# Both mixers in two kinds of visits, copies back in place, and a head of joint weight tiles

## What is computed

```
z = rmsnorm(x, g_mix) @ w_in                       # 2048 -> 5632 columns, split among the heads
mixer A: 16 heads x 64; each evaluates three (window, dilation) patterns (128,1), (512,4), (2048,16),
         with ALiBi; the three outputs are mixed by their softmax denominators
mixer B: 16 query heads / 4 kv heads x 64; keys t-128..t, ALiBi, a sink logit in the denominator
h = x + concat(oa * silu(ga), ob * silu(gb)) @ w_out
y = h + (p @ w_ple) * sigmoid(rmsnorm(h, g_ple) @ w_pg);  final rmsnorm
```

## Time and profile before

| | |
|---|---|
| median of 3 runs | 2344.28 us (2338.28 to 2345.48) |
| the profiled execution | 2341.7 us |
| its span, first to last instruction | 2339.9 us |
| TensorE busy | 2278.0 us (97%), mean granted clock 0.995 |
| VectorE, ScalarE, POOL busy | 905.0 us, 565.0 us, 771.8 us |
| TensorE busy in the first 65 us | 34.6 us |
| TensorE busy from 135 to 900 us | 765.0 us of 765.0 |

### The profile page before, as it was taken

How to read it: one execution, slowest core, us unless ns; L and a number is a source line. 1 busy time by engine, 2 the same in 40 slices (tenths; PEclk the granted TensorE clock), 3 DMA queues, 4 the chain that set the end, 5 groups by cost and what they waited for, 6 DMA issues and landing times.

```text
span 2339.9 us, 39175 instructions
## 1 busy us (share of the span) xinstructions
PE 2278.0 (97%) x15570; PEld 2179.3 (93%) x15570; DVE 905.0 (39%) x2334; ACT 565.0 (24%) x1562; POOL 771.8 (33%) x783
## 2 busy tenths in 40 slices
PE   4999999999999999999999999999999999999996
PEld 4999999999999999999988999899999999999996
DVE  7123333333324413455555424343233373222235
ACT  5122222222222212323544310210000030000374
POOL 2232222222222133222222233343333344555564
PEclk9999999999999999999999999999999999999998
DMA  5144454444444425455464454454343555444666
GB/s 196 61 125 96 104 117 96 108 114 96 109 111 96 107 71 147 131 147 146 138 160 142 135 174 131 158 139 111 86 102 92 122 164 133 113 115 109 194 202 224
DMA packets 542140, 299.71 MB, mean 128 GB/s; under 512 B 245140, under 2 KB 507300, under 8 KB 540668
## 3 DMA queue, kind: packets, MB, share of 16 engines
q1 hardware_dynamic: 464277, 254.82, 41.1%
q10 hardware_dynamic: 77680, 42.39, 6.3%
HBM read 230.76 MB, written 66.36 MB: 127 GB/s over the span
## 4 chain that ended last, share of the span: by engine, by line
PE 90%; DVE 4%; DMA 2%; ACT 2%; POOL 1%; issue 0%; SPq 0%; DVEq 0%; ACTq 0%; POOLq 0%
PE psum L1081 26%; PE psum L1083 26%; PE psum L1082 26%; PE psum L889 3%; PE psum L911 2%; PE psum L922 2%; PE psum L951 1%; PE psum L979 1%; PE psum L966 1%; DMA h_stage<-h_scratch 1%; DVE x_n L1554 1%; DVE act_lo L1545 1%; PE psum L986 1%; POOL w_lo L845 0%; DMA x_in<-in_x_prompt 0%; DVE act_lo L1912 0%
## 5 line engine op out<-in xcount | busy, mean ns | idle before, releaser
L1081 PE MATMUL psum<-act_hi,w_hi 128*128 128x344 f32 x4032 | 1303.4, 323 | 6.6 <-POOL w_lo L845 5.3
L1083 PE MATMUL psum<-act_hi,w_lo 128*128 128x344 f32 x4032 | 1286.9, 319 | 0.0
L1082 PE MATMUL psum<-act_lo,w_hi 128*128 128x344 f32 x4032 | 1286.1, 319 | 0.0
L1081 PEld LDWEIGHTS psum<-act_hi,w_hi 128*128 128x128 f32 x4032 | 758.2, 188 | 17.9 <-issue 12.4
L1083 PEld LDWEIGHTS psum<-act_hi,w_lo 128*128 128x128 f32 x4032 | 757.5, 188 | 0.0
L1082 PEld LDWEIGHTS psum<-act_lo,w_hi 128*128 128x128 f32 x4032 | 757.2, 188 | 0.2
L843 POOL CAST w_hi<-w_raw 128x512 fp32r<-128x512 f32 (+1 forms) x352 | 222.8, 633 | 1464.1 <-PE psum L1083 1274.9
L845 POOL TENSOR_TENSOR w_lo<-w_raw,w_hi 128x512 fp32r<-128x512 f32 (+1 forms) x390 | 508.7, 1306 | 59.6 <-ACT w_hi L1488 31.3
L1657 DVE COPY prob_t<-psum 128x512 f32<-128x512 f32 (+1 forms) x56 | 35.5, 634 | 391.5 <-PE psum L922 391.5
L1958 DVE TENSOR_TENSOR t_gate<-psum,acc 128x344 f32<-128x344 f32 x48 | 24.7, 515 | 224.9 <-PE psum L1083 224.9
L1889 DVE TENSOR_TENSOR h_row<-psum,h_row 128x344 f32<-128x344 f32 x48 | 22.1, 513 | 212.9 <-PE psum L1083 212.9
(11 more groups left out here) (208 smaller groups left out, 1787.4 us busy)
## 6 DMA issues: line engine op xcount, KB each, us to landing
w_raw<-in_w_in SPq DMA_DIRECT2D x208, 256.0 KB, 3.0
w_raw<-in_w_pg SPq DMA_DIRECT2D x94, 256.0 KB, 2.8
w_raw<-in_w_out SPq DMA_DIRECT2D x64, 256.0 KB, 2.7
z_scratch<-stage ACTq DMA_DIRECT2D x72, 172.0 KB, 1.9
h_scratch<-h_row ACTq DMA_DIRECT2D x16, 516.0 KB, 2.7
x_in<-in_x_prompt SPq DMA_DIRECT2D x8, 1024.0 KB, 5.1
zq<-z_scratch SPq DMA_DIRECT2D x32, 256.0 KB, 3.9
out<-z_sq SPq DMA_DIRECT2D x128, 64.0 KB, 2.8
```

Source lines behind the costliest of these rows:

```text
L1081: pe.matmul(psum[:, bank, 0:T3], hi_w, hi_a[:, k, rows], start=(k == 0), stop=False, skip_group_check=True)
L1082: pe.matmul(psum[:, bank, 0:T3], hi_w, lo_a[:, k, rows], start=False, stop=False, skip_group_check=True)
L1083: return pe.matmul(psum[:, bank, 0:T3], lo_w, hi_a[:, k, rows], start=False, stop=stop, skip_group_check=True)
```

## The change

- **Mixer A, two kinds of visits.** Chunks 1 and 2, and 3 and 4, are scored in one visit. A pair has eight steps in 144 positions; at even ones TensorE does values and then scores (positions 0, 36, 72, 108 of the pair), at odd ones turns alone (22, 58, 94, 130). A chunk scored at step s is turned at s + 1 (the far chunk, scored at 0, at 7), and its values are done at the next even step. Scores and turns of a chunk use the same PSUM banks (2 and 3, or 4 and 5: `A_SLOT`); outputs collect in banks 6 and 7.
- **Copies back in place.** The turned columns are copied into `prob` where the chunk stood; `prob_t` and `probt_b` are gone, and `prob` has one set of places instead of two.
- **Mixer B.** Four blocks (`BQ`) in a visit: values and scores at steps 0 and 4, turns at 3 and 7. The scores of four blocks go head by head for two blocks each, no longer block by block.
- **Head.** x has three buffers and is normed in place. Three row tiles are turned first; the first unit does high x high and high x low for all k, and low x high behind them. The first two column tiles are walked jointly, third by third. Eight groups of weights are split ahead (three more places, `w_hi_head`, `w_lo_head`). `pick` is issued ahead of `g_row`.
- SP's squares of low values get an event of their own (`a_low`), `zv`'s low half is loaded a step earlier, and `sink` and `kb` share semaphores with other tables.

The diff, cut to its core:

```diff
-X_FIRST = 4
-X_LATER = {4: 4, 8: 5, 13: 6, 19: 7, 27: 8}
+X_FIRST = 3
+X_LATER = {12: 3, 17: 4, 26: 5, 39: 6, 44: 7, 48: 8}
+X_BANKS = 24
+LO_AFTER = {1: (0,), 2: (1, 2), 4: (3,), 5: (4, 5), 7: (6,)}
+HEAD_TILES = 2
+HEAD_UNITS = [(i, t) for t in range(3) for i in range(HEAD_TILES)]
+HEAD_BANKS = [0, 1, 6, 7, 0, 1]
...
 A_COLS = [512, 512, 384, 512, 384, 384, 512]
 NCH = len(A_PARTS)
-SCORE_AT = [0, 2, 3, 4, 5, 6, 8]
-TURN_AT = [7, 4, 5, 6, 8, 9, 10]
-TURN_ORDER = [1, 2, 3, 0, 4, 5, 6]
-SCALE_AT = [6, 3, 4, 5, 6, 7, 9]
-SCALE_ORDER = [1, 2, 3, 4, 0, 5, 6]
...
-PLACE_FREE = [(-1, 3), (-1, 4), (-1, 5), (-1, 6), (0, 1), (0, 2), (0, 0)]
-A_STEPS = 13
+A_HALVES = 8
+A_STEPS = 12
+SCORE_AT = [0, 2, 2, 4, 4, 6, 8]
+SCORED_WITH = [0, 1, 1, 3, 3, 5, 0]
+TURN_AT = [7, 3, 3, 5, 5, 7, 9]
+TURN_ORDER = [1, 2, 3, 4, 0, 5, 6]
+SCALE_ORDER = [1, 2, 3, 4, 5, 0, 6]
+A_SLOT = [0, 0, 1, 0, 1, 1, 1]
+PLACE = [0, 4, 8, 4, 8, 4, 4]
+PLACE_FREE = [(-1, 0), (-1, 6), (-1, 4), (0, 1), (0, 2), (0, 3), (0, 5)]
 SQUARE_AT = [1, 2, 4, 6]
...
+TURN_B, VALUES_B = 3, 4
+B_BANKS = (2, 3, 4, 7)
 SETS = [(1920, 1, 128), (1536, 4, 96), (0, 16, 96)]
...
-    for g in range(7, WG * (NZ - 2) + 7):
-        tile, part = divmod(g - 7, WG)
-        put(16 * (3 * tile + 2) + 4 * (part + 1), "weights", g)
+    for g in range(HEAD_GROUPS + 2, WG * (NZ - 2) + 7):
+        tile, part = divmod(ring_before(g - 2), WG)
+        put(16 * last_unit(tile) + 4 * (part + 1), "weights", g)
     for u in range(GATE0, ZPAIR):
         put(16 * u + 5, "o_load", u)
     put(152, "a_load")
     for n in range(PAIRS):
-        for s in range(NCH if n + 1 < PAIRS else A_STEPS):
-            put(176 + 144 * n + (144 * s // NCH if n + 1 < PAIRS else 14 * s), "a", n, s)
+        for s in range(A_HALVES if n + 1 < PAIRS else A_STEPS):
+            put(176 + 144 * n + (36 * (s // 2) + 22 * (s % 2) if n + 1 < PAIRS else 32 * (s // 2) + 20 * (s % 2)), "a", n, s)
+        put(176 + 144 * n + 50, "a_low", n)
...
-                if i >= 2:
-                    sp.wait_ge(sem("x_normed"), i - 1)
-                sp.dma_start(x_in[0:n, i % 2, :], x_p[r0:r0 + n, :] if i < 8 else x_s).then_inc(sem(f"x_loaded{i % 2}"), 16)
+                if i >= 3:
+                    sp.wait_ge(sem("x_turned"), 4 * (i - 2))
+                sp.dma_start(x_in[0:n, i % 3, :], x_p[r0:r0 + n, :] if i < 8 else x_s).then_inc(sem(f"x_loaded{i % 3}"), 16)
                 if i == 0:
                     sp.dma_start(ident[:], a["c_ident"]).then_inc(sem("consts"), 16)
+                    sp.dma_start(pick[:], a["c_pick"]).then_inc(sem("consts"), 16)
                     sp.wait_ge(sem("x_loaded0"), 16)
                     sp.dma_start(g_row[:], bcast_rows(a["g_mix"][0:1, :], P)).then_inc(sem("consts"), 16)
-                elif i == 1:
-                    sp.dma_start(pick[:], a["c_pick"]).then_inc(sem("consts"), 16)
...
+                for g in {2: (0, 1), 3: (2, 3), 4: (4, 5), 5: (6, 7)}.get(i, ()):
                     weights(g)
-            for g in range(5, 7):
+            for g in range(HEAD_GROUPS, HEAD_GROUPS + 2):
...
                         store_squares(n, V_HIGH)
+                        load_zv(n, 0)
                         sp.wait_ge(sem("fstat_stored"), 16 * (n + 1))
                         sp.dma_start(n_stat[:, n % 2].rearrange("p m h b -> p (m h) b"), fs_dram[n % 2].rearrange("m (b p) -> p m b", p=P),
                                      allow_slow_non_contiguous=True).then_inc(sem("nstat_loaded"), 16)
...
-                        if more:
-                            load_zv(n + 1, 1)
                         store_squares(n, K_LOW)
                     elif s == 8 and more:
+                        load_zv(n + 1, 1)
...
             def a_scores(n, c):
-                first = scored_before(n, c)
+                first, bank = scored_before_step(n, c), 2 + 2 * A_SLOT[c]
...
-                        if i == 0 and first:
-                            pe.wait_ge(sem("a_biased"), 2 * (first - 1) + h + 1)
-                        mm = pe.matmul(psum[:, 2 + h, col:col + w], queries(half), keys(half), start=True, stop=True)
+                        if i == 0 and h == 0 and first:
+                            pe.wait_ge(sem("a_biased"), 2 * first)
+                        mm = pe.matmul(psum[:, bank + h, col:col + w], queries(half), keys(half), start=True, stop=True)
...
-                        mm = pe.matmul(psum[HD * h:HD * h + HD, 6, c0:c1:step], values[:, HD * h:HD * h + HD], prob_t[:, h, x * P:(x + 1) * P],
+                        mm = pe.matmul(psum[HD * h:HD * h + HD, bank, c0:c1:step], values[:, HD * h:HD * h + HD], prob_of(c)[:, h, x * P:(x + 1) * P],
...
-                before = turned_before(n, c)
+                before, bank = turned_before(n, c), 2 + 2 * A_SLOT[c]
...
             def a_step(n_, s_):
                 for n, s in a_walked(n_, s_):
-                    if s in SCORE_AT:
-                        a_scores(n, SCORE_AT.index(s))
+                    for c in TURN_ORDER:
+                        if TURN_AT[c] == s - 1:
+                            a_values(n, c)
+                for n, c in a_chunks(n_, s_):
+                    a_scores(n, c)
                 for n, s in a_walked(n_, s_):
-                    if s - 1 in TURN_AT:
-                        a_values(n, TURN_AT.index(s - 1))
-                for n, s in a_walked(n_, s_):
-                    if s in TURN_AT:
-                        a_turns(n, TURN_AT.index(s))
+                    for c in TURN_ORDER:
+                        if TURN_AT[c] == s:
+                            a_turns(n, c)
...
-                    for x, b in enumerate((s_, s_ + 1)):
-                        k0, nk = max(b - 1, 0) * BLK, BLK * min(b + 1, 2)
-                        for h in range(2):
-                            half = slice(HD * h, HD * h + HD)
-                            if x == 0 and (n_ or s_):
-                                pe.wait_ge(sem("b_biased"), QB * n_ + s_ + h - 1)
-                            mm = pe.matmul(psum[:, 2 + h, 256 * x:256 * x + nk], zq[half, b * BLK:(b + 1) * BLK], zkb[half, k0:k0 + nk],
-                                           start=True, stop=True)
-                            if x:
-                                mm.then_inc(sem("b_scored"), 1)
...
+                    for two in range(0, BQ, 2):
+                        for h in range(2):
+                            half = slice(HD * h, HD * h + HD)
+                            for x, b in enumerate((s_ + two, s_ + two + 1)):
+                                k0, nk = max(b - 1, 0) * BLK, BLK * min(b + 1, 2)
+                                mm = pe.matmul(psum[:, B_BANKS[two + h], 256 * x:256 * x + nk], zq[half, b * BLK:(b + 1) * BLK], zkb[half, k0:k0 + nk],
+                                               start=True, stop=True)
+                            mm.then_inc(sem("b_scored"), 1)
...
+            def first_unit():
+                rows = slice(0, T3)
+                pe.wait_ge(sem("x_hi"), 4 * 3)
+                for k in range(KT):
+                    if k in X_LATER:
+                        x_turn(X_LATER[k])
+                    group_wait("in", 0, k)
+                    hi_w, lo_w = split_place(GROUP["in", 0, k - k % WG], WG)
+                    pe.matmul(psum[:, 0, 0:T3], hi_w[:, k % WG, :], act_hi[:, k, rows], start=(k == 0), stop=False, skip_group_check=True)
+                    pe.matmul(psum[:, 0, 0:T3], lo_w[:, k % WG, :], act_hi[:, k, rows], start=False, stop=False, skip_group_check=True)
+                pe.wait_ge(sem("x_lo"), 4 * 3)
+                for k in range(KT):
+                    hi_w = split_place(GROUP["in", 0, k - k % WG], WG)[0]
+                    mm = pe.matmul(psum[:, 0, 0:T3], hi_w[:, k % WG, :], act_lo[:, k, rows], start=False, stop=(k == KT - 1), skip_group_check=True)
+                mm.then_inc(sem("produced"), 1)
             for i in range(X_FIRST):
                 x_turn(i)
             for u in range(ZPAIR):
-                tile, t = divmod(u, 3)
-                if u < 3:
-                    pe.wait_ge(sem("x_lo"), 4 * (3, 6, len(ROW_TILES))[u])
+                tile, t = unit_of(u)
+                if u == 0:
+                    first_unit()
+                    continue
+                if tile == 0:
+                    pe.wait_ge(sem("x_lo"), 4 * (3, 6, len(ROW_TILES))[t])
                 for k in range(KT):
                     for e in EVENTS.get(16 * u + k, ()):
                         beside(e)
...
-                if i >= 1:
-                    x_lo_parts(i - 1)
+                for split in LO_AFTER.get(i, ()):
+                    x_lo_parts(split)
+            x_lo_parts(7)
             x_lo_parts(8)
...
             def a_step(n_, s_):
+                if s_ == SQUARE_AT[V_LOW]:
+                    turn_squares(n_, V_LOW)
                 for n, s in a_walked(n_, s_):
-                    for part, at_s, ended in ((0, 9, A_FAR), (1, 12, NCH - 1)):
```

(8 more changed lines are left out.)

351 lines of the change are left out of this document (187 added, 164 removed).

## The result

| | before | after |
|---|---|---|
| median of the runs | 2343.9 us | 2380.3 us |
| ratio, 95% interval | | 1.016 (1.014 to 1.018) |
| profiled execution, its span | 2341.7, 2339.9 us | 2382.5, 2380.7 us |
| mean granted clock of TensorE | 0.995 | 0.986 |

Forecast were 2318 us and a gain; it is a loss of 36 us, 62 us away from the forecast. This is what experiments have to explain.

What follows compares the result with a forecast made beforehand. TensorE, busy 97%, was taken as the bound. From the profiled 2341.7 us, 19 for visits and 7.3 for the head came off, giving 2315.4; with 2.6 added, the median forecast was 2318 us, range 2308 to 2335 (8 in 10).

Steps and rivals of the forecast that it cites:

- Other queues: Loads, stores and POOL: reordering costs zero; zv's load makes DVE 1 us late at step 2, covered by slack.
- rival 1: Mixer windows: look-ahead becomes a wait; 0.7 us late in each of 48 windows gives 2352 us; chance 0.09.
- Copies back in place ... zero: Turned columns copied into prob instead of prob_t: same instructions and shapes, no TensorE wait to remove, zero.
- The visits, gain 19: Both mixers: overhead paid per visit falls from 47.3 to 28.0 us; gain 19 us, between 10 and 25.
- The head, gain 7.3: Kernel start: first main at 28 us, 144 mains done by last turn at 67.3; gain 7.3 us, bounds 3 to 10.
- Order of the scores, zero: Mixer B: two blocks of one head, then the other's, still overlap because TensorE overtakes; cost zero.
- Rivals 2: Mixer B's scores: nothing overlaps, 27 us lost, 2345 us; chance 0.09.
- Rival 3: Mixer B's scores: matmuls keep program order, only neighbours overlap, about 7 us lost, 2325 us; chance 0.12.
- The sum: Whole kernel: 2341.7 - 19 - 7.3 = 2315.4 us profiled, 2.6 more for a median: 2318 us.
- the far weights' 3: Mixer A's far chunk: weights sent through DRAM are back 3 us before their turns, so no TensorE wait.

Runs made afterwards that it cites:

- e3: Changed kernel with zv's low half turned behind the biases on VectorE and n_stat issued ahead of the stores and zv's load on SP: 2353.1 us.
- e5: Changed kernel with zv's low half turned last, n_stat loaded first, and no wait for copies inside a visit of turns: 2338.4 us, ratio 0.998 to before.
- e4: Changed kernel without the wait of a chunk's turns for the copies of the chunk turned before (a_copied): 2364.1 us.
- e6: e5 with the decode work beside mixer B every 80 positions instead of 90, its last two steps at 80 and 85: 2324.4 us, ratio 0.992.
- e7: e6 with mixer B's scores alternating between the heads block by block, as in the kernel before: 2321.5 us, ratio 0.991.
- experiment 5: Comparison of mixer B's score orders: e6 (heads two blocks at a time) at 2324.4 us against e7 (heads alternating) at 2321.5 us.
- e10: Label not defined in the text; apparently the changed kernel with only n_stat issued ahead of the stores and zv's load on SP: 2397.3 us.

## Why the prediction was wrong, step by step

**"DVE is 1 us late, which the slack of two microseconds at that step (rival 1) covers" (Other queues).** This is the step that failed worst: 27 us (after against e3). The place had been seen, and the new order of `zv` on VectorE named with what stands behind it. The sizes were off. `zv` was put 10.4 us behind the start of step 1's turns; it landed 12.6 us behind (510.48 to 523.04). The hand count started SP's work when TensorE's step starts, and SP got to it 3.2 us later, behind a weight load that waits for POOL; that such loads "keep their positions" was said, and that SP stands in them was not. The second need of the same step, `n_stat`, was not in the count at all. And the slack was used up by something else: VectorE's wait ended about 2.1 us behind the scores, and in seven pairs 2.6 to 5 us arrived at TensorE with the slow turns in between (1.0 in the first). The rows say where the slack went. From the first bias to the first turn it takes 10.0 to 10.4 us in pairs two to six, and TensorE is back 10.4 us after the scores. In each of these pairs two of the first chunk's four scales run beside POOL and take 1.7 to 2.2 us together, in place of 0.7. In e3, where the biases start with the scores, all four are done before POOL comes, at 0.35 us each. So the hand count's two microseconds were about right for scales that run alone, and with POOL beside them 0.0 to 0.4 us of it was left. "On POOL nothing but the weights runs" was said; that the weights slow VectorE was not in the sum. This reading rests on the traces; no run takes POOL away.

**Rival 1** is thus what happened, by another road. It priced a wait in each of 48 windows; one window in each pair was late, by 2.6 to 5 us in seven pairs, and the others fitted, as the prediction's chain had it (e3 and e5: no wait at all of mixer A's turns for VectorE). Its 2352 is 28 us short of the measured 2380, and its chance of 0.09 was far too low for a cover of 0.5 to 3 us that rests on a hand count over three queues.

**"Copies back in place ... zero".** The copies are free as such; nothing in e5's mixer A is left for them to cost, though they were not tried alone. What the step missed stands beside them in the code: the wait for `a_copied` between chunks stayed in `a_turns` when two chunks came into one visit. 16.2 us (after against e4), 14.8 (e3 against e5). It was visible in the new code, and the prediction counted what leaves a visit and not what two chunks in one visit do to each other.

**Mixer B.** The prediction had no term for the decode work. It cost 14.0 us (e5 against e6), because ScalarE and VectorE get twice the work at once at half the rate, in positions that the decode work shares. Busy shares of 39 and 24% told nothing of that.

**The visits, gain 19.** Right in the price of a visit; what arrived as time is less certain. A visit of values and scores has 0.545 us over in mixer A (31 visits of after, median; 0.55 was taken), turns alone have 0.002 to 0.01. One such visit in the changed kernel, 28 passes of values and 384 keys:

```profile
194.14 0.32 PE L1156 MATMUL psum<-act_hi,w_lo 128*128 128x344 f32 x1
194.39 1.75 PE L984 MATMUL psum<-prob,v_nat 128*64 128x128 f32 x28
196.07 0.92 PE L962 MATMUL psum<-zk,zq 64*128 64x384 f32 x4
...
197.18 0.32 PE L1155 MATMUL psum<-act_lo,w_hi 128*128 128x344 f32 x1
```

In the prediction's terms: 3.04 - 0.31 - 28 x 0.055 - 0.64 = 0.55 us over.

Once the waits are out, mixer A is 9.0 us and mixer B 9.5 us faster than before in the profiled execution of e7, 18.5 of the 19. That execution is 6.7 us below e7's median, though. In e6, profiled near its median, the two are 8.1 and 4.4 us, with 1.6 lost to the scores' order and 2.5 to slow mains in mixer B. Three changes of kind cost 0.545 us here, where they cost 0.52 in the earlier trace rows; what it is in a change that costs time, no row shows.

**The head, gain 7.3.** 5.2 us in the profiled execution. The first main starts at 29.85 us and not at 28. VectorE's part of the hand count holds (third tile's turns from 25.49, forecast 25.1); the turns themselves do not:

```profile
25.49 3.68 PE L934 MATMUL psum<-ident,x_in 128*128 128x128 f32 x16 [2.86 <-DVE x_in L1641]
29.85 0.66 PE L1171 MATMUL psum<-act_hi,w_hi 128*128 128x344 f32 x1 [0.69 <-ACT act_hi L1349]
...
68.09 0.46 PE L1154 MATMUL psum<-act_hi,w_hi 128*128 128x344 f32 x1
```

Sixteen turns take 3.68 us, 0.23 each and not 0.11, after 2.86 us of standing idle, and the mains behind them start every 0.29 us until 34 us: that is the pace that they have at a granted clock of 0.50 from 536.96 to 539.25 us. (The view of this trace gives a clock of 1.00 for the stretch, which the pace contradicts; e7's gives 0.50 from 26.1 to 32.8 us.) The last turn ends at 68.1 us with 144 mains done (67.3 was forecast), and the mains behind it start every 0.29 us for a while again: 1.6 us of the gain are lost there (-6.8 at main 144, -5.2 at main 200).

**Order of the scores, zero.** Nearly: 1.6 us. Rivals 2 (27) and 3 (6.8) are out. Rival 3 would give one pass pair more a visit, 0.43 us; the rows show 0.10. Its premise, that matmuls keep the program's order, no row shows; the pairs of experiment 5, 0.013 us apart with three passes of the other head between them in the program, speak against it.

**The sum.** From the forecast of 2318 to the measured 2380: 27 for `zv` and `n_stat`, 15 for the copies inside a visit, 14 for the decode work, 3 for the scores' order (by medians; by the visits 1.6), and 3 that stay (two of them the head's): e7 stands at 2321.5. As far as the rows show, no price of TensorE's own work was off by more than some 2 us; every large term was a wait.

## What to carry to other kernels

When work is bundled so that a bottleneck engine changes its kind of work less often, price the bundles on the other engines too: each gets its work in larger lumps, and whatever stands behind a lump in an engine's program comes later by it (in e5 TensorE waited up to 3.1 us for `s_prob`). List for every visit all that must have landed (loads on the same queue, one behind the other, included), start the count where that queue really is, not where the program's position is, and take a cover below some 3 us for no cover (the two microseconds of step 3 were 0.0 to 0.4, the far weights' 3 about zero). Price a chain at what its instructions take beside the engines that will run then, not at what they take alone (0.89 us against 0.35 for a scale of 128 x 256 here). And look for waits written for one item a visit that now stand between two items of the same visit.

## What the runs showed of the hardware that was not expected

- **The clock falls with the waits, and not for the wait alone.** In the changed kernel 117 times two neighbouring mains start 0.27 to 0.30 us apart and not 0.157, 15 us in all; in the kernel before 5 times, 0.7 us. 37 of them are in mixer A, in seven groups of 1 to 8, each behind one of the seven waits of 1.85 to 3.5 us there; the eighth wait, 1.2 us, has none behind it. e7, without these waits, has none in either mixer. The length of a wait alone does not decide: waits of 1.85 to 1.9 us had slow mains behind them in mixer A of the changed kernel and in e6, and two of 1.88 us in e7 had none. The list of waits alone understates such a stall: 2.6 us at 534.05 had 1.1 us more behind it in eight mains, and the last six of the turns in between were slow too.
- **VectorE's scales slow down beside POOL.** In mixer A of the changed kernel the in-place scale of 128 x 256 (L1675) takes 0.35 us where no POOL instruction overlaps it (28 of them) and 0.89 us on average, up to 1.45, where one does (20). A copy out of PSUM beside POOL takes what it takes alone (L1741, 0.69 us for 512 columns both ways). A row beside the waiting turns of step 3, and POOL at the same time:

```profile
530.70 2.10 DVE L1675 TENSOR_SCALAR prob<-prob,near 128x256 f32<-128x256 f32 x2
530.70 0.61 POOL L916 CAST w_hi<-w_raw 128x512 fp32r<-128x512 f32 x1
531.39 1.26 POOL L918 TENSOR_TENSOR w_lo<-w_raw,w_hi 128x512 fp32r<-128x512 f32 x1
...
533.38 0.61 DVE L1675 TENSOR_SCALAR prob<-prob,near 128x256 f32<-128x256 f32 x2
```

  The two scales that take 0.61 us at 533.38 took 2.10 at 530.70. In e3 and e7 the first chunk's scales of step 3 come before POOL's work and take 0.35 us each. No run here takes POOL away, so this is a reading of traces. Slowed are the scales, which read and write `prob` (0.35 to 0.89 us), and not the copies out of PSUM (0.69 us both ways); the cause of it is in no row.
- **A small scattered load slows what is issued behind it on the queue.** Behind 8 KB of `n_stat` four stores of 64 KB took 5.18 us to issue, without it ahead of them 3.14. It is the first issue behind the load that is long, 3.55 of the 5.18 us; the three others took 0.49 to 0.51. The same holds in all eight pairs of the kernel before, the changed one, e3 and e10: whatever is issued right behind `n_stat` takes 1.1 to 4.5 us.
